# Sums of squares of the query and key heads: one exact fp32 product against two fp32r products, taken two weight pieces later

## The chip, the cores and the metric

One NeuronCore of a Trainium2 chip runs the whole program in one launch. The metric is device time in microseconds. The engines are PE (TensorE), ACT (ScalarE), DVE (VectorE), POOL (GpSimd) and SP (SyncE, which here only issues transfers). Each executes its own instruction list in order, and they meet through semaphores.

## The reference, cut to what matters

Two transformer blocks run one after the other on 256 tokens of width 2048 in float32. The change is in the first block, where the input projection gives queries and keys for two attentions of 8 heads each, and every head is normalised over its 128 elements:

```python
proj = h @ w_in
qa, ka, va, za, q_idx, k_idx, w_idx, qb, kb, vb, zb = jnp.split(proj, COL_SPLITS, axis=-1)
qa = _rms_norm(qa.reshape(heads_a), q_norm_a)
ka = _rms_norm(ka.reshape(heads_a), k_norm_a)
# the same for qb and kb
# _rms_norm: x * rsqrt(mean(x * x, axis=-1) + 1e-6) * g
```

In the kernel a head lies with its 128 elements on the 128 partitions and the 256 tokens along the free axis. The sum over the elements of a head is therefore a sum over partitions. It is made on PE, as a product of the squares with a 128x128 matrix of ones, which also puts the sum on every partition.

## The kernel before, in words

**Weights in pieces.** A projection is cut into panels of 512 output columns (4 PSUM banks of 128), and a panel into 8 pieces of 128x1024 (two blocks of 128 rows). SP loads a piece into one of 4 slots (`raw`). ACT rounds it to fp32r (`w_hi`, line 1193). DVE subtracts that from the original (`w_lo`, line 1698). PE makes three fp32r products per block and bank (lines 764 to 766), 24 for a piece. Piece j uses slot j mod 4, so ACT rounds piece j+4 when PE has released piece j, and DVE can't make `w_lo` of a piece before ACT has made its `w_hi`. PE must have `w_lo` of a piece before it starts it.

**Hooks.** All other work is put behind numbered pieces of a panel, in the instruction list of each engine. A hook at 4 on ACT stands behind ACT's rounding of piece 4. A hook at 2 on PE stands behind PE's products of piece 2. An engine which waits in a hook does not go on to its next piece.

**The stage.** The panels in question are `qk_a` (4 panels, queries and keys of the first attention), `v_a` (2), `qk_b` (4) and `v_b` (2). The results of a panel are taken out while the next panel runs. So the squares are made eight times: in panels 1 to 3 of `qk_a` (a loop of three turns), panel 0 of `v_a`, panels 1 to 3 of `qk_b` (a loop of three turns) and panel 0 of `v_b`. One time is called a turn below. It goes so:

- ACT hook 2, `stored`: copies each bank to the store and squares it into `sq` (128x1024), then frees the bank.
- PE hook 0, `qk_sums` (line 838): two products of `ones` with the halves of `sq`, in fp32, into `Y`. Each shows as two records of the trace.
- ACT hook 4, `qk_rstd`: waits for these sums (`ss_ready`), then Ln, Exp and Square over 128x1024 (lines 1207 to 1209).
- DVE hook 5, `qk_norm`: a refinement of three operations (lines 1692, 1713, 1714), then the scaling of the heads. The third operation raises `rs_ready`.

**What else stands at these places.** In `qk_a`: PE hooks 0 and 3 are index logits (line 855); ACT hooks 5 and 7 are relus of them; DVE hooks 5 and 7 sum them up (`index_sum`, in front of `qk_norm`), and DVE hooks 3 and 6 are `gate_sum` (128x2048). In `v_a` DVE has a `pick` (a step of a top-64 selection) at hooks 1, 3, 5 and 7. In `qk_b` the attention of two heads of the first kind runs as well: PE has `score` at 0, `v_rows` at 3, `probs_t` at 4 and `values` at 6; ACT has `exps` at 5 and `probs_a` at 7; DVE has `softmax_in` at 4, `softmax_out` at 6 and `probs_d` at 7. There `v_rows` writes into `Y`, and so it waits until `rs_ready` says that the refinement of the same turn has read `Y`; `probs_t` waits for `softmax_out`. In `v_b` DVE has `gate_sum` at 1, 3 and 5.

Of the kernel before, what the change touches and what calls it, by code (L numbers as in the profile page):

```python
# [28 lines left out]
P = 128  # L29
D = 2048  # L30
DC = D // P
SEQ = 256
# [128 lines left out]
def memory(nc, ctx, A):  # L161
# [6 lines left out]
    def put(name, shape, dt=FP32, offset=None):  # L168
        size = int(np.prod(shape[1:])) * 4
        here = at["o"] if offset is None else offset  # L170
        t = nc.alloc_sbuf_tensor_at(name, list(shape), dt, offset=here)
        end = here + (size + 31) // 32 * 32
        if offset is None:
            at["o"] = end
        assert end <= nc.sbuf_usable_end, name
        M.end = end
        return t
# [73 lines left out]
    M.dist = put("dist", [P, 384], offset=x + 20480)  # L251
    M.dist_sel = put("dist_selected", [P, 384], offset=x + 22016)
    M.k_idx = put("k_idx_twice", [P, SEQ], offset=x + 23552)


    M.qkv = put("qkv", [P, 24 * ROWS], offset=q0)
# [53 lines left out]
    def sem(name):  # L310
        return ctx.enter_context(nc.semaphore(name))
# [18 lines left out]
    M.y2_ready = sem("y2_ready")  # L330
    M.rs_ready = sem("rs_ready")
    M.norm_done = sem("norm_done")
    M.src_ready = sem("src_ready")
    M.ahi_ready = sem("ahi_ready")
    M.act_ready = sem("act_ready")
# [398 lines left out]
def pe_program(M, pe):  # L734
# [5 lines left out]
    def panel(job, i, after={}, acts=None, pair=None, value=None, opened={}):  # L740

        acc, ready, free = (M.acc, M.acc_ready, M.acc_free) if value is None else (M.val, M.val_ready, M.val_free)
        stored = [n + (i if pair is None else pair) for n in job.free0] if value is None else [value] * 4
        for j in range(job.J):
            s = j % SLOTS
            pe.wait_ge(M.lo_ready[s], job.raw0 + job.turn(i, j) + 1)
            if acts is not None:
                pe.wait_ge(M.act_ready, acts + job.kp * (j + 1))  # L750
            for b in job.banks:
                col = 0 if len(job.banks) == 1 else b * P
                out = acc[b][:, 0:job.N]
                if j == 0:
                    at_least(pe, free[b], stored[b])
                    if b in opened:
                        opened[b]()
                for k in range(job.kp):
                    c = job.kp * j + k
                    last = c == job.kp * job.J - 1  # L760
                    a_hi, a_lo = job.rhs(c)
                    w_hi = M.hi[s][:, k * job.cols + col:k * job.cols + col + P]
                    w_lo = M.lo[s][:, k * job.cols + col:k * job.cols + col + P]
                    pe.matmul(out, w_lo, a_hi, start=c == 0, stop=False)  # L764
                    pe.matmul(out, w_hi, a_lo, start=False, stop=False)  # L765
                    ins = pe.matmul(out, w_hi, a_hi, start=False, stop=last)  # L766
                if j == job.J - 1:
                    ins.then_inc(ready[b], 1)
            if j < job.J - 1:
                ins.then_inc(M.used[s], 1)  # L770
            for step in after.get(j, ()):
                step()
# [58 lines left out]
    panel(job["qidx1"], 0, {0: [k_idx_sums], 5: [k_idx_twice]})  # L831


    def qk_sums(stored):
        def go():
            pe.wait_ge(M.acc_free[3], stored)
            for t in range(2):
                ins = pe.matmul(M.Y[:, t * 512:(t + 1) * 512], ones[:, 0:P], M.sq[:, t * 512:(t + 1) * 512],
                                start=True, stop=True)
            ins.then_inc(M.ss_ready, 1)  # L840
        return go

# [17 lines left out]

    a = job["qk_a"]
    panel(a, 0, {0: [logits(0, 0)], 3: [logits(0, 1)]})
    with pe.Fori(0, a.n - 1) as i:
        panel(a, i + 1, {0: [qk_sums(a.free0[3] + i + 1), logits(i + 1, 0)], 3: [logits(i + 1, 1)]})
    panel(job["v_a"], 0, {0: [qk_sums(a.free0[3] + 4)]})
    panel(job["v_a"], 1)


# [50 lines left out]

    def hooks(u, k_off, norms, sums=()):  # L920
        score, v_rows, probs_t, values = unit(u, k_off, norms)
        return {0: [*sums, score], 3: [v_rows], 4: [probs_t], 6: [values]}

    b = job["qk_b"]
    k_a, k_b = 16 * SEQ, 40 * SEQ
    panel(b, 0, hooks(0, k_a, 6))
    with pe.Fori(0, b.n - 1) as i:
        panel(b, i + 1, hooks(i + 1, k_a + (i + 1) * 512, i + 7, (qk_sums(b.free0[3] + i + 1),)))
    panel(job["v_b"], 0, {0: [qk_sums(b.free0[3] + 4)]})
    panel(job["v_b"], 1)  # L930

    def gate_cols():
# [233 lines left out]
def act_program(M, act):  # L1166
# [28 lines left out]
    def panel(job, i, after={}, before={}, pair=None, part=0):  # L1195

        for j in range(job.J):
            for step in before.get(j, ()):
                step()
            split(job, i, j, pair, part)  # L1200
            for step in after.get(j, ()):
                step()
# [75 lines left out]
    act.activation(M.cc[:, 3 * CT:4 * CT], M.Y[:, 128:128 + CT], ACT.Copy)  # L1278
    act.activation(M.cc[:, 0:3 * CT], M.Y[:, 640:640 + 3 * CT], ACT.Copy).then_inc(M.cols, 1)
    act.wait_ge(M.cols, 2)  # L1280
    act.activation(M.bqkv[:, 0:8], M.c2[:, V2_QKV:V2_QKV + 8], ACT.Copy, scale=HD ** -0.5)
    act.activation(M.bqkv[:, 8:24], M.c2[:, V2_QKV + 8:V2_QKV + 24], ACT.Copy)
    ch.step(act.activation(M.bgate[:, :], M.c2[:, V2_UG + 8:V2_UG + 40], ACT.Copy, scale=0.5), wait=False)
# [5 lines left out]
        return M.act2_hi[:, PITCH * k + ROWS - n:PITCH * k + ROWS]  # L1289


    def stored(job, i, tile, func=ACT.Copy, squares=None):


        def go():
            for m in range(4):
                act.wait_ge(M.acc_ready[m], job.ready0[m] + i + 1)
                dst = M.store[:, ds(tile * SEQ + m * SEQ, SEQ)]
                ins = act.activation(dst, M.acc[m][:, 0:SEQ], func)
                if squares is not None:  # L1300
                    if m == 0:
                        act.wait_ge(M.rs_ready, squares)
                    ins = act.activation(M.sq[:, m * SEQ:(m + 1) * SEQ], M.acc[m][:, 0:SEQ], ACT.Square)
                ins.then_inc(M.acc_free[m], 1)
        return go

    q0, strip, q1 = job["qidx0"], job["strip"], job["qidx1"]
# [66 lines left out]
    def out_stored(u, at):  # L1374
        def go():
            act.wait_ge(M.o_ready, u + 1)
            act.activation(M.store[:, ds(at, 512)], M.Y[:, 512:1024], ACT.Copy).then_inc(M.o_done, 1)
        return go
# [2 lines left out]
    panel(b, 0, {2: [stored(job["v_a"], 1, 28)], 5: [exps(0)], 7: [probs_a(0)]})  # L1381
    with act.Fori(0, b.n - 1) as i:
        ch.enter(i, 2)
        panel(b, i + 1, {2: [out_stored(i, qa + i * 512), stored(b, i, 32 + i * 4, squares=i + 6)],
                         4: [qk_rstd(i + 6, i + 4)], 5: [exps(i + 1)], 7: [probs_a(i + 1)]})
        ch.leave(b.n - 1)
    panel(job["v_b"], 0, {2: [out_stored(3, qa + 3 * 512), stored(b, 3, 44, squares=9)], 4: [qk_rstd(9, 7)]})
    panel(job["v_b"], 1, {2: [stored(job["v_b"], 0, 48)]})
    za, zb = job["z_a"], job["z_b"]
    panel(za, 0, {2: [stored(job["v_b"], 1, 52)], 5: [exps(4)], 7: [probs_a(4)]})  # L1390
# [294 lines left out]
def dve_program(M, dve):  # L1685
# [114 lines left out]
    def qk_norm(count, at, gain):  # L1800
# [4 lines left out]
            stt(part, part, M.gqk[:, ds(gain, 1)], M.rs[:, :], ALU.mult, ALU.mult).then_inc(M.norm_done, 1)  # L1805
        return go

    def index_sum(u, tile, first=False):

        def go():  # L1810
            if first:
                dve.wait_ge(M.score_zero, 1)
            dve.wait_ge(M.rl_ready, 2 * u + tile + 1)
            for half in range(2):
                ch.wait()
                for t in range(2):
                    n = (t + 1) * P
                    part = M.idx_score[:, t * P:t * P + n]
                    col = t * IDX_HEADS + 2 * tile + half
                    ins = stt(part, M.relu[:, half * 384 + t * P:half * 384 + t * P + n],  # L1820
                              M.w_idx[:, ds(4 * u + col, 1)], part, ALU.mult, ALU.add)
                    if half == 0 or t == 0:
                        ch.step(ins, wait=False)
                    else:
                        ins.then_inc(M.rl_used, 1)
            dve.wait_ge(M.rl_used, 2 * u + tile + 1)
        return go
# [3 lines left out]
                 7: [index_sum(0, 1)]})  # L1831
    with dve.Fori(0, a.n - 1) as i:
        ch.enter(i, 8)
        panel(a, i + 1, {3: [gate_sum(0, i + 2, 2 * i + 4)],
                         5: [index_sum(i + 1, 0), qk_norm(i + 3, (i + 2) * 4 * SEQ, i)],
                         6: [gate_sum(1, i + 2, 2 * i + 5)], 7: [index_sum(i + 1, 1)]})
        ch.leave(a.n - 1)
# [14 lines left out]
        ch.step(dve.tensor_scalar(M.work[:, :], M.work[:, :], SENTINEL / 2, NEG, ALU.is_gt, ALU.mult))  # L1852
        ch.step(dve.tensor_tensor(M.dist_sel[:, :], M.work[:, :], M.dist[:, :], ALU.add))

    panel(job["v_a"], 0, {1: [candidates, pick], 3: [pick], 5: [qk_norm(6, 20 * SEQ, 3), pick], 7: [pick]})
    panel(job["v_a"], 1, {1: [pick], 3: [pick], 5: [pick], 7: [pick, selected]})


# [35 lines left out]
    panel(b, 0, hooks(0, 0, M.dist_sel))  # L1894
    with dve.Fori(0, b.n - 1) as i:
        ch.enter(i, 5)
        panel(b, i + 1, hooks(i + 1, 2 * i + 2, M.dist_sel, [qk_norm(i + 7, (i + 8) * 4 * SEQ, i + 4)]))
        ch.leave(b.n - 1)

    def gates(n):  # L1900
        return gate_sum(n % 2, n // 2, n)

    panel(job["v_b"], 0, {1: [gates(10)], 3: [gates(11)], 5: [gates(12), qk_norm(10, 44 * SEQ, 7)]})
    panel(job["v_b"], 1, {1: [gates(13)], 3: [gates(14)], 5: [gates(15)]})

    def gate():
# [316 lines left out]
```

## Time and profile before

| | |
|---|---|
| time, median of 3 runs | 2095.51 us (2095.13 to 2096.24) |
| profiled execution, its own time | 2093.64 us |
| its span | 2091.8 us |
| PE busy | 1980.5 us, 95% of the span |
| DVE busy | 1308.3 us, 63% |
| ACT busy | 991.2 us, 47% |
| mean granted PE clock | 0.974 |

Times of rows are microseconds from the start of the span. In a timeline row stand the start, the duration, the engine, the line, the operation and its tiles, and in brackets how long the engine was idle before it and what ended that. In a row of the chain (the work that ended last, followed back) stand the start, the time that this link held the chain, the engine and the tile. In a windows row stand the stretch, its length, then for each engine the busy time and the number of instructions, then the granted PE clock as a share of full speed, the DMA share and the GB/s. The modelled duration of a matmul overlaps the next one, so the time that PE needs is read from starts.

### The profile page before, as it was taken

The page shows a single profiled execution, that of the slowest core. Times are in us where ns is not written, and L with a number is a line of the kernel's source. Part 1 is how long each engine was busy: PE and PEld are TensorE (multiplying, and loading weights), DVE is VectorE, ACT ScalarE, POOL GpSimd, SP SyncE. Part 2 cuts the span into 40 slices and gives each one's busy share as a digit, 9 for nine tenths or more (in the row PEclk, how much of TensorE's full clock was granted, in tenths as well). Part 3 has the DMA queues.
Part 4 walks back from the last instruction along what each step waited for, and adds up shares of the span by engine and source line. Part 5 has one row for each costly group of instructions (what it writes and reads, how often), then busy time and mean ns, then how long its engine had stood idle before and what let it go on. Part 6 is the DMA issues. An engine that isn't in the chain of part 4 may idle for free.

```text
span 2091.8 us, 39050 instructions
## 1 busy us (share of the span) xinstructions
PE 1980.5 (95%) x15084; PEld 1882.8 (90%) x15084; DVE 1308.3 (63%) x1647; ACT 991.2 (47%) x1430; POOL 139.3 (7%) x149
## 2 busy tenths in 40 slices
PE   4289999999999999999999999799999999999997
PEld 2289999999998999998889999799999999988885
DVE  7886886675666544444447653676677667665554
ACT  3055555554645544444444544644454454444443
POOL 0000000000002000000004111000001000000000
PEclk8599999999999999999999999899999999999999
DMA  9966664474455455544444555256555655655553
GB/s 376 355 204 239 246 200 158 159 283 146 151 188 182 151 180 165 177 141 143 140 138 151 201 183 180 72 187 200 186 170 179 200 183 170 204 208 189 191 191 121
DMA packets 179903, 391.62 MB, mean 187 GB/s; under 512 B 11955, under 2 KB 17632, under 8 KB 177376
## 3 DMA queue, kind: packets, MB, share of 16 engines
q1 hardware_dynamic: 178800, 388.03, 55.5%
q10 hardware_dynamic: 1024, 2.51, 0.3%
q8 instruction: 54, 0.88, 0.2%
q14 instruction: 25, 0.20, 0.0%
HBM read 388.39 MB, written 2.10 MB: 187 GB/s over the span
## 4 chain that ended last, share of the span: by engine, by line
PE 90%; DVE 6%; ACT 2%; issue 1%; DMA 1%; SPq 0%; DVEq 0%; POOLq 0%; POOL 0%; ACTq 0%
PE acc L764 21%; PE acc L765 20%; PE acc L766 20%; PE psum_x L764 2%; PE psum_y L765 2%; PE psum_x L765 2%; PE psum_x L766 2%; PE psum_y L766 2%; PE psum_y L764 2%; DVE ada_acc L1692 2%; PE acc L1145 2%; PE acc L1144 2%; PE acc L1146 2%; DVE ada_first L1692 2%; PE psum_y L1145 1%
## 5 line engine op out<-in xcount | busy, mean ns | idle before, releaser
L1698 DVE TENSOR_TENSOR w_lo<-raw,w_hi 128x1024 fp32r<-128x1024 f32 (+1 forms) x644 | 810.0, 1271 | 655.2 <-ACT w_hi L1193 652.5
L1193 ACT ACTIVATE w_hi<-raw 128x1024 fp32r<-128x1024 f32 (+1 forms) x644 | 672.6, 1051 | 837.0 <-PE acc L766 547.6
L764 PE MATMUL acc<-act_hi,w_lo 128*128 128x258 f32 (+2 forms) x3424 | 976.1, 285 | 19.3 <-issue 11.1
L765 PE MATMUL acc<-act_lo,w_hi 128*128 128x258 f32 (+2 forms) x3424 | 965.3, 282 | 0.0
L766 PE MATMUL acc<-act_hi,w_hi 128*128 128x258 f32 (+2 forms) x3424 | 965.0, 282 | 0.0
L764 PEld LDWEIGHTS acc<-act_hi,w_lo 128*128 128x128 f32 x3424 | 648.9, 190 | 30.5 <-issue 28.7
L765 PEld LDWEIGHTS acc<-act_lo,w_hi 128*128 128x128 f32 x3424 | 648.0, 189 | 0.7 <-issue 0.5
L766 PEld LDWEIGHTS acc<-act_hi,w_hi 128*128 128x128 f32 x3424 | 648.1, 189 | 0.0
L764 PE MATMUL psum_x<-act_hi,w_lo 128*128 128x258 f32 x352 | 99.8, 283 | 4.1 <-DVE w_lo L1698 4.1
L765 PE MATMUL psum_x<-act_lo,w_hi 128*128 128x258 f32 x352 | 99.6, 283 | 0.0
L764 PE MATMUL psum_y<-act_hi,w_lo 128*128 128x258 f32 x352 | 99.6, 283 | 0.0
L765 PE MATMUL psum_y<-act_lo,w_hi 128*128 128x258 f32 x352 | 99.6, 283 | 0.0
L766 PE MATMUL psum_x<-act_hi,w_hi 128*128 128x258 f32 x352 | 99.6, 283 | 0.0
L766 PE MATMUL psum_y<-act_hi,w_hi 128*128 128x258 f32 x352 | 99.6, 283 | 0.0
L764 PEld LDWEIGHTS psum_x<-act_hi,w_lo 128*128 128x128 f32 x352 | 66.9, 190 | 4.5 <-DVE w_lo L1698 4.5
L725 POOL TENSOR_TENSOR ffn_act<-gelu_gate,conv_val 128x1024 f32 x11 | 35.2, 3201 | 524.6 <-DVE conv_val L1692 524.6
L1145 PE MATMUL acc<-w_lo,down_hi 128*128 128x512 f32 x176 | 69.3, 394 | 0.0
L1144 PE MATMUL acc<-w_hi,down_lo 128*128 128x512 f32 x176 | 69.0, 392 | 0.0
L1146 PE MATMUL acc<-w_hi,down_hi 128*128 128x512 f32 x176 | 68.3, 388 | 0.0
L765 PEld LDWEIGHTS psum_x<-act_lo,w_hi 128*128 128x128 f32 x352 | 66.9, 190 | 0.0
L765 PEld LDWEIGHTS psum_y<-act_lo,w_hi 128*128 128x128 f32 x352 | 66.8, 190 | 0.0
L766 PEld LDWEIGHTS psum_y<-act_hi,w_hi 128*128 128x128 f32 x352 | 66.8, 190 | 0.0
(296 smaller groups left out, 2207.8 us busy)
## 6 DMA issues: line engine op xcount, KB each, us to landing
raw<-in_w_in SPq DMA_DIRECT2D x272, 512.0 KB, 3.5
raw<-in_w_ffn_up SPq DMA_DIRECT2D x176, 512.0 KB, 4.4
raw<-in_w_ffn_down SPq DMA_DIRECT2D x88, 512.0 KB, 3.6
raw<-in_w_out SPq DMA_DIRECT2D x64, 512.0 KB, 4.1
raw<-in_w_ada SPq DMA_DIRECT2D x32, 512.0 KB, 8.3
ada_w<-in_w_ada SPq DMA_DIRECT2D x32, 512.0 KB, 8.0
ada_x<-in_w_ada SPq DMA_DIRECT2D x16, 1024.0 KB, 6.2
raw<-in_w_attn_o SPq DMA_DIRECT2D x16, 512.0 KB, 3.6
```

Of the source, the lines that this page charges most:

```text
L725: pool.tensor_tensor(M.F[:, ds(i * 4 * SEQ, 4 * SEQ)], M.gg[:, :], M.vt[:, :], ALU.mult).then_inc(M.F_ready, 1)
L764: pe.matmul(out, w_lo, a_hi, start=c == 0, stop=False)
L765: pe.matmul(out, w_hi, a_lo, start=False, stop=False)
L766: ins = pe.matmul(out, w_hi, a_hi, start=False, stop=last)
L1144: pe.matmul(out, d_lo, w_hi, start=start, stop=False)
L1145: pe.matmul(out, d_hi, w_lo, start=False, stop=False)
L1146: ins = pe.matmul(out, d_hi, w_hi, start=False, stop=stop)
L1193: act.activation(M.hi[s][:, 0:job.width], M.raw[s][:, 0:job.width], ACT.Copy).then_inc(M.hi_ready[s], 1)
L1692: return dve.scalar_tensor_tensor(out, in0, scalar, in1, op0, op1)
L1698: dve.tensor_tensor(M.lo[s][:, 0:job.width], M.raw[s][:, 0:job.width], M.hi[s][:, 0:job.width].bitcast(FP32), ALU.subtract).then_inc(M.lo_ ...
```

## The change

Four things are done, each eight times.

- ACT, at the end of `stored`, copies `sq` rounded to fp32r into a new tile `sq_hi` (128x1024). Before it, it waits for its own last square.
- DVE has a new hook at 2, `square_low`: it waits for that copy and subtracts it from `sq`, giving `sq_lo` (128x1024, fp32r).
- PE makes, for each half, two fp32r products of a rounded matrix of ones, with `sq_lo` and with `sq_hi`, in place of the fp32 product. That is four products with 512 columns.
- These products stand at PE hook 2 in place of hook 0, and wait for `square_low` in place of the freed bank.

The hooks of `qk_rstd` (ACT 4) and `qk_norm` (DVE 5) stay. Once, early in the program, ACT makes the rounded ones. The new tiles lie in parts of the store that are empty at the time. No transfer is added or moved.

```diff
-    def qk_sums(stored):
+    def qk_sums(n, side):
         def go():
-            pe.wait_ge(M.acc_free[3], stored)
+            pe.wait_ge(M.sql_ready, n + 1)
             for t in range(2):
-                ins = pe.matmul(M.Y[:, t * 512:(t + 1) * 512], ones[:, 0:P], M.sq[:, t * 512:(t + 1) * 512],
-                                start=True, stop=True)
+                out, part = M.Y[:, t * 512:(t + 1) * 512], slice(t * 512, (t + 1) * 512)
+                pe.matmul(out, M.ones_r[:, :], M.sq_lo[side][:, part], start=True, stop=False)
+                ins = pe.matmul(out, M.ones_r[:, :], M.sq_hi[side][:, part], start=False, stop=True)
             ins.then_inc(M.ss_ready, 1)
...
-        panel(a, i + 1, {0: [qk_sums(a.free0[3] + i + 1), logits(i + 1, 0)], 3: [logits(i + 1, 1)]})
-    panel(job["v_a"], 0, {0: [qk_sums(a.free0[3] + 4)]})
+        panel(a, i + 1, {0: [logits(i + 1, 0)], 2: [qk_sums(i, 0)], 3: [logits(i + 1, 1)]})
+    panel(job["v_a"], 0, {2: [qk_sums(3, 0)]})
...
-        return {0: [*sums, score], 3: [v_rows], 4: [probs_t], 6: [values]}
+        return {0: [score], 2: list(sums), 3: [v_rows], 4: [probs_t], 6: [values]}
...
-        panel(b, i + 1, hooks(i + 1, k_a + (i + 1) * 512, i + 7, (qk_sums(b.free0[3] + i + 1),)))
-    panel(job["v_b"], 0, {0: [qk_sums(b.free0[3] + 4)]})
+        panel(b, i + 1, hooks(i + 1, k_a + (i + 1) * 512, i + 7, (qk_sums(i + 4, 1),)))
+    panel(job["v_b"], 0, {2: [qk_sums(7, 1)]})
...
+    act.activation(M.ones_r[:, :], M.ones[:, 0:P], ACT.Copy).then_inc(M.ones_ready, 1)
...
+            if squares is not None:
+                act.wait_ge(M.acc_free[3], job.free0[3] + i + 1)
+                act.activation(M.sq_hi[side][:, :], M.sq[:, :], ACT.Copy).then_inc(M.sqh_ready, 1)
...
+    def square_low(n, side):
+
+        def go():
+            dve.wait_ge(M.sqh_ready, n + 1)
+            dve.tensor_tensor(M.sq_lo[side][:, :], M.sq[:, :], M.sq_hi[side][:, :].bitcast(FP32), ALU.subtract
+                              ).then_inc(M.sql_ready, 1)
+        return go
...
-        panel(a, i + 1, {3: [gate_sum(0, i + 2, 2 * i + 4)],
+        panel(a, i + 1, {2: [square_low(i, 0)], 3: [gate_sum(0, i + 2, 2 * i + 4)],
```

The hook of `square_low` at 2 is added in the same way in panel 0 of `v_a`, in the loop of `qk_b` and in panel 0 of `v_b`.

## Rows read from the trace of the kernel before

**Rows 1.** The windows: one turn of `qk_a` and one of `qk_b`.

```profile
192.58:218.21 25.63, 25.63 (x213) 23.60 (x213) 21.34 (x23) 15.37 (x21) 1.19 (x1) 1.00 0.56 205
...
369.67:398.65 28.98, 28.13 (x223) 26.62 (x223) 18.81 (x26) 17.11 (x29) 1.72 (x2) 1.00 0.46 145
```

**Rows 2.** The chain in a turn of `qk_a`: sums, logits, three pieces, logits.

```profile
192.58 1.72 PE psum_y L838 x4
194.29 0.86 PE psum_x L855 x8
...
203.53 0.86 PE psum_x L855 x8
```

**Rows 3.** The timeline of ACT in the same turn.

```profile
196.64 1.07 ACT L1209 ACTIVATE squares<-rstd 128x1024 f32<-128x1024 f32 x1
198.19 1.06 ACT L1193 ACTIVATE w_hi<-raw 128x1024 fp32r<-128x1024 f32 x1 [0.48 <-PE acc L766]
```

**Rows 4.** The timeline of DVE in the same turn.

```profile
199.28 1.23 DVE L1698 TENSOR_TENSOR w_lo<-raw,w_hi 128x1024 fp32r<-128x1024 f32 x1 [2.88 <-ACT w_hi L1193]
...
202.09 1.22 DVE L1692 SCALAR_TENSOR_TENSOR squares<-psum_y,squares 128x1024 f32<-128x1024 f32 x1
...
206.78 1.21 DVE L1698 TENSOR_TENSOR w_lo<-raw,w_hi 128x1024 fp32r<-128x1024 f32 x1
...
213.38 3.50 DVE L1698 TENSOR_TENSOR w_lo<-raw,w_hi 128x1024 fp32r<-128x1024 f32 x3 [0.44 <-DVE idx_score L1692]
```

**Rows 5.** The page's costliest groups: the subtraction and the rounding of a piece.

```profile
L1698 DVE TENSOR_TENSOR w_lo<-raw,w_hi 128x1024 fp32r<-128x1024 f32 (+1 forms) x644 | 810.0, 1271 | 655.2 <-ACT w_hi L1193 652.5
L1193 ACT ACTIVATE w_hi<-raw 128x1024 fp32r<-128x1024 f32 (+1 forms) x644 | 672.6, 1051 | 837.0 <-PE acc L766 547.6
```

**Rows 6.** The windows: 20 us of the last stage, fp32r products of 512 columns.

```profile
1900.00:1920.00 20.00, 20.00 (x89) 16.39 (x89) 9.65 (x11) 9.13 (x12) 0.00 (x0) 1.00 0.53 187
```

**Rows 7.** The timeline of ACT in panel 0 of `v_a`.

```profile
273.52 1.06 ACT L1209 ACTIVATE squares<-rstd 128x1024 f32<-128x1024 f32 x1
274.49 1.05 ACT L1193 ACTIVATE w_hi<-raw 128x1024 fp32r<-128x1024 f32 x1
```

**Rows 8.** The timeline of DVE in panel 0 of `v_a`.

```profile
275.57 1.23 DVE L1698 TENSOR_TENSOR w_lo<-raw,w_hi 128x1024 fp32r<-128x1024 f32 x1 [1.08 <-ACT w_hi L1193]
276.71 1.22 DVE L1692 SCALAR_TENSOR_TENSOR squares<-psum_y,squares 128x1024 f32<-128x1024 f32 x1
...
282.85 2.36 DVE L1698 TENSOR_TENSOR w_lo<-raw,w_hi 128x1024 fp32r<-128x1024 f32 x2
```

**Rows 9.** The timeline of DVE in panel 0 of `v_b`.

```profile
434.47 2.35 DVE L1692 SCALAR_TENSOR_TENSOR ada_acc<-ada_x,silu_c,ada_acc 128x2048 f32<-128x2048 f32 x1
...
441.18 5.04 DVE L1698 TENSOR_TENSOR w_lo<-raw,w_hi 128x1024 fp32r<-128x1024 f32 x4
```

**Rows 10.** The chain in a turn of `qk_b`.

```profile
371.38 1.31 PE psum_x L881 x8
372.69 0.12 PE acc L764
...
377.85 1.23 DVE squares L1692
...
379.83 1.24 DVE rstd L1714
...
382.54 1.63 DVE w_lo L1698
...
385.36 0.88 PE psum_x L775 x6
```

**Rows 11.** The windows: two idle stretches of PE, and PE's work right behind each.

```profile
1307.81:1314.17 6.36, 0.00 (x1) 0.03 (x1) 4.74 (x10) 3.09 (x8) 0.00 (x0) 0.77 0.00 0
1314.17:1318.05 3.88, 3.88 (x18) 3.88 (x19) 3.81 (x7) 1.91 (x4) 0.00 (x0) 0.50 0.01 2
1349.57:1353.70 4.13, 0.00 (x0) 0.00 (x1) 1.28 (x2) 4.00 (x7) 0.00 (x0) 0.82 0.00 0
1353.70:1359.02 5.32, 5.32 (x24) 5.32 (x25) 4.63 (x9) 4.25 (x7) 0.00 (x0) 0.50 0.31 99
```

More of the change, by code:

```diff
@@ L253, in memory @@
     M.k_idx = put("k_idx_twice", [P, SEQ], offset=x + 23552)
+    M.ones_r = put("ones_rounded", [P, P], F32R, x + 24576)
+    M.sq_hi = [put(f"squares_hi{n}", [P, 4 * SEQ], F32R, store(part)) for n, part in enumerate((4, 0))]
+    M.sq_lo = [put(f"squares_lo{n}", [P, 4 * SEQ], F32R, store(part) + 4096) for n, part in enumerate((4, 0))]
     M.qkv = put("qkv", [P, 24 * ROWS], offset=q0)
@@ L332, in memory @@
     M.norm_done = sem("norm_done")
+    M.ones_ready = sem("ones_ready")
+    M.sqh_ready = sem("sqh_ready")
+    M.sql_ready = sem("sql_ready")
     M.src_ready = sem("src_ready")
@@ L862, in pe_program @@
     panel(a, 0, {0: [logits(0, 0)], 3: [logits(0, 1)]})
+    pe.wait_ge(M.ones_ready, 1)
     with pe.Fori(0, a.n - 1) as i:
-        panel(a, i + 1, {0: [qk_sums(a.free0[3] + i + 1), logits(i + 1, 0)], 3: [logits(i + 1, 1)]})
-    panel(job["v_a"], 0, {0: [qk_sums(a.free0[3] + 4)]})
+        panel(a, i + 1, {0: [logits(i + 1, 0)], 2: [qk_sums(i, 0)], 3: [logits(i + 1, 1)]})
+    panel(job["v_a"], 0, {2: [qk_sums(3, 0)]})
     panel(job["v_a"], 1)
@@ L1289, in hi2_of, with stored @@
         return M.act2_hi[:, PITCH * k + ROWS - n:PITCH * k + ROWS]
-    def stored(job, i, tile, func=ACT.Copy, squares=None):
+    def stored(job, i, tile, func=ACT.Copy, squares=None, side=0):
         def go():
@@ L1383, in act_program @@
         ch.enter(i, 2)
-        panel(b, i + 1, {2: [out_stored(i, qa + i * 512), stored(b, i, 32 + i * 4, squares=i + 6)],
+        panel(b, i + 1, {2: [out_stored(i, qa + i * 512), stored(b, i, 32 + i * 4, squares=i + 6, side=1)],
                          4: [qk_rstd(i + 6, i + 4)], 5: [exps(i + 1)], 7: [probs_a(i + 1)]})
         ch.leave(b.n - 1)
-    panel(job["v_b"], 0, {2: [out_stored(3, qa + 3 * 512), stored(b, 3, 44, squares=9)], 4: [qk_rstd(9, 7)]})
+    panel(job["v_b"], 0, {2: [out_stored(3, qa + 3 * 512), stored(b, 3, 44, squares=9, side=1)], 4: [qk_rstd(9, 7)]})
     panel(job["v_b"], 1, {2: [stored(job["v_b"], 0, 48)]})
@@ L1853, in selected @@
         ch.step(dve.tensor_tensor(M.dist_sel[:, :], M.work[:, :], M.dist[:, :], ALU.add))
-    panel(job["v_a"], 0, {1: [candidates, pick], 3: [pick], 5: [qk_norm(6, 20 * SEQ, 3), pick], 7: [pick]})
+    panel(job["v_a"], 0, {1: [candidates, pick], 2: [square_low(3, 0)], 3: [pick], 5: [qk_norm(6, 20 * SEQ, 3), pick], 7: [pick]})
     panel(job["v_a"], 1, {1: [pick], 3: [pick], 5: [pick], 7: [pick, selected]})
@@ L1896, in dve_program @@
         ch.enter(i, 5)
-        panel(b, i + 1, hooks(i + 1, 2 * i + 2, M.dist_sel, [qk_norm(i + 7, (i + 8) * 4 * SEQ, i + 4)]))
+        panel(b, i + 1, {2: [square_low(i + 4, 1)],
+                         **hooks(i + 1, 2 * i + 2, M.dist_sel, [qk_norm(i + 7, (i + 8) * 4 * SEQ, i + 4)])})
         ch.leave(b.n - 1)
@@ L1901, in gates @@
         return gate_sum(n % 2, n // 2, n)
-    panel(job["v_b"], 0, {1: [gates(10)], 3: [gates(11)], 5: [gates(12), qk_norm(10, 44 * SEQ, 7)]})
+    panel(job["v_b"], 0, {1: [gates(10)], 2: [square_low(7, 1)], 3: [gates(11)], 5: [gates(12), qk_norm(10, 44 * SEQ, 7)]})
     panel(job["v_b"], 1, {1: [gates(13)], 3: [gates(14)], 5: [gates(15)]})
```

## The prediction

> **What bounds the kernel now.** I read the page first. PE is busy for 95% of the span, so a microsecond that PE loses in this stage is lost at the end too, unless it shortens an idle stretch that PE has anyway. Then I took the windows from sums to sums. In a turn of `qk_a` PE is busy for all of the 25.63 us and DVE for 21.34; in a turn of `qk_b` PE has less than 1 us idle in 28.98 [rows 1]. Then came the chain: in `qk_a` it stays on PE [rows 2], and in `qk_b` it leaves PE once a turn, for ACT's rounding and then DVE's refinement, `w_lo` and softmax, until PE can transpose the probabilities [rows 10]. Last I read the timelines of ACT and DVE, to see who is how late in a turn. The question for this change is how much slack lies between the end of the sums (called S below) and the first piece on PE that needs what ACT and DVE do behind their hooks 4 and 5.
>
> **PE's own work.** Before, the fp32 sums hold PE for 1.72 us [rows 2]. The four new products have 512 columns, and fp32r products of that width come 89 in 20 us, 0.225 us each [rows 6]: 0.90 us. That gives back 0.82 us a turn. The bounds: not under four products of half the width (72 of them fill the 8.38 us of three pieces below, 0.116 each: 0.47 us), and not over the 1.72 of the fp32 form, so between 0 and 1.25 us a turn. I take 0.82, since the rows have the same type and width.
>
> **The added passes.** ACT's copy is as large as a rounding, 1.05 us, and DVE's subtraction as a `w_lo`, 1.27 us with its spread [rows 5]. They stand before the split of piece 3, and PE needs that only after its pieces 0 to 2, some 8 us later. In `qk_a` DVE's busy time would go from 21.34 to about 22.5 of 24.8 us. I cost both at nothing while pieces 1 and 2 cover them; without cover they would cost 2.3 us a turn. The rounded ones are made once, long before the stage, and cost nothing.
>
> **The move is what costs.** On ACT hook 4 `qk_rstd` waits for the sums, and behind it on ACT stands the rounding of piece 5. Before, the sums end at 194.29 [rows 2], ACT begins its last step of `rstd` at 196.64, and the rounding of piece 5 comes at 198.19, released by PE and not by `rstd` [rows 3]. The wait was free. Now the sums end two pieces later, and ACT stands still at hook 4 with piece 5 unrounded, DVE behind it. From S on all turns share a chain:
> - S to the rounding of piece 5: 2.35 us to the Square (194.29 to 196.64, rows 2 and 3), then 0.97 [rows 7]: S+3.32.
> - DVE takes up `w_lo` of piece 5 1.08 later, S+4.40, and is through 1.14 later [rows 7, 8]: S+5.54.
>
> After S, PE has work for piece 3, piece 4 and piece 5. In `qk_a` three pieces last 195.15 to 203.53, 8.38 us [rows 2].
>
> **A turn of `qk_a` (three).** DVE needs 2.81 us from `w_lo` 5 over `index_sum` to `qk_norm` and 4.69 more until `w_lo` of piece 6 starts [rows 4]: S+11.90, ready at S+13.17. PE has 8.38 and the logits' 0.86 [rows 2], so it arrives at S+9.24 and waits 3.93 us. DVE stays late: `w_lo` of the next panel's piece 0 starts 6.60 after that of piece 6 [rows 4], ready at S+19.75, while PE would be there two pieces (5.5) after S+13.17; another 1.1 us. With the 0.82 back: 4.2 us a turn, 12.6 for three.
>
> **`v_a` (one).** From S+5.54 DVE needs 6.14 for `qk_norm` and `pick` (276.71 to 282.85, rows 8): `w_lo` 6 ready at S+12.95. PE has 8.38, waits 4.57; net 3.75.
>
> **A turn of `qk_b` (three).** The refinement starts at S+5.54 and its third step ends 3.21 later (377.85 to 379.83, and 1.23, rows 10): S+8.75. `v_rows` behind piece 3 waits for it. PE comes there at S+2.8, so it waits 5.9 us. The rest of the chain, 4.69 to `w_lo` and 2.82 to the transposes [rows 10], sets `probs_t` at S+13.05. Before, it stood at S+13.98 (371.38 to 385.36), but with `score` (1.31) and pieces 1 and 2 (5.6) between. These 6.9 us now stand ahead of S, so a turn changes by 13.05 - 13.98 + 6.9 - 0.82 = 5.15, 15.5 for three.
>
> **`v_b` (one).** From S+5.54, `gate_sum` and `qk_norm` take 6.71 [rows 9]: `w_lo` 6 ready at S+13.5, PE waits 5.1, net 4.3.
>
> Sum at full clock: 12.6 + 3.75 + 15.5 + 4.3 = 36.2 us. Bounds: with the products at either bound it is 32.8 to 42.8. No link of it is a resource that the trace does not show.
>
> **The clock.** PE stands idle for 6.36 us and for 4.13 us near 1310 and 1350. In both the granted clock falls before PE goes on, and PE then works 3.88 and 5.32 us at 0.50, which is 1.2 GHz and not 2.4 [rows 11]. Half of that, 1.9 to 2.7 us, is lost; I take 2.3. The waits of `v_a`, `qk_b` and `v_b` (4.6, 5.9, 5.1) are longer than 4.13, so I count a fall in each. Those of `qk_a` (3.9) are a little shorter; I count one in two. What it costs: in `v_a` and `v_b` the full 2.3. In `qk_b`, `v_rows` and piece 4 end at S+14.4 and not S+12.1, past the 13.05 of `probs_t`: 1.35 a turn, 4.05. In `qk_a` the slow piece hides the second wait of 1.1: 1.2 a turn, 1.8 for three at one in two. Together 10.45; bounds: 0 without any fall, 15.5 with 2.7 lost at each of eight.
>
> The Trainium skill ("TensorE: Matmul & The Clock Gate", section "HAM oscillation — how this bites in real kernels") says that a kernel whose matmuls wait once in each iteration can fall back to the slow clock every time. By it every one of the eight waits has a fall; by the rows alone that is sure for five. It speaks against a change that makes waits.
>
> **Forecast.** 36.2 + 10.45 = 46.6 us. Against the profiled execution, 2093.64, that gives 2140.3; the median of the runs is 1.87 above it, so 2095.51 + 46.6 = 2142.1 us.
>
> **Rivals.**
> - *Clock stays up.* The waits are there, but PE's dense work around them keeps the clock. For it: the idle stretches of rows 11 stand beside small fp32 products, those here between dense pieces. Against: they are as long. 36.2 us: 2131.7.
> - *A fall at each of the eight.* 46.6 + 1.8 = 48.4: 2143.9, and with the longer slow stretches (2.7) 2148. That is inside the forecast's own range.
> - *Late loads on top.* SP issues the load of a slot when `w_lo` has left it, so DVE's lateness makes loads late. It decides if a piece lands after ACT could round it. The DMA share in these turns is 0.46 to 0.56 [rows 1], which speaks against. At 1 us a turn: +8, 2150.
> - *The other side: the chain has slack that I don't see.* If PE found `w_lo` 6 and `rs_ready` on time, only the 0.82 of each turn would be left: 8 x 0.82 = 6.6, 2088.9. It decides where ACT's hook 4 would have to end two pieces earlier than S+3.3, and nothing in the change moves that hook. The same comes out if the busy share were the judge (DVE 22.5 of 24.8 us).
> - *Partly hidden.* DVE or ACT save some of the chain because they have less to do while PE waits: the waits at full clock are 36.2 + 6.6 = 42.8 us, half of them less the 6.6 is +14.8, 2110.3.
>
> **How the numbers follow.** Forecast with five to eight falls 0.60 (its own range 2137 to 2149); clock stays up 0.20; late loads 0.10; partly hidden 0.07; waits all hidden 0.03. The range takes in the second and most of the third: 2127 to 2152. A difference under 0.2% (4.2 us) can't be told from none. Slower by more has all but the last case and a rest: 0.96; no change 0.01; faster 0.03.
>
> **What would show each step.** Each PE group of line 838's successor holds PE for 0.9 us. ACT is idle some 5 us before Ln in each turn, released by PE's sums. PE is idle near 4 us before piece 6 in `qk_a`, released by `w_lo`; near 5.9 us before `v_rows` in `qk_b`, released by DVE's `rstd`. The turn of `qk_a` is 30 to 31 us, that of `qk_b` 34 to 35.5. The clock shows 0.50 behind the waits. The forecast is wrong if ACT rounds piece 5 without waiting for the sums, or if the granted clock stays at 1.00.

## The result, and the profile after

The changed kernel takes 2140.65 us (median of 4 runs, 2138.72 to 2142.02) against 2095.32 for the kernel before. The ratio is 1.0218, with a 95% interval of 1.0205 to 1.0231: 45 us slower. Its profiled execution has a span of 2136.9 us, where before had 2091.8, and a mean granted clock of 0.967, where before had 0.974. PE's busy share fell from 95% to 93%. All ratios here and below are of fast runs; of the kernels below one run, 2229 us at a granted clock of 0.83, was in the chip's slow state.

First the waits of PE in the stage, from 180 to 520 us: who waited for whom, the total, how often, and the longest.

```profile
PE psum_y L781 <- DVE rstd L1726: 17.8, 3, 5.9
PE acc L770 <- DVE w_lo L1710: 13.7, 9, 4.7
PE psum_x L862 <- ACT relu_logits L1351: 6.8, 3, 2.3
```

Before, PE waited 2.1 us for the probabilities here and hardly for anything else. Now it waits 38.3 us. The first row is `v_rows` in the three turns of `qk_b`, 5.9 us each. The second is mostly piece 6 (4.7 us in `v_b`, 4.3 in `v_a`, 0.4 to 1.6 in the turns of `qk_a`). The third is one that the prediction did not name: the second index logits of `qk_a`, 2.3 us in each of its turns.

Second, ACT in the first turn of `qk_a`, in the timeline; these answer to [rows 3].

```profile
201.03 1.12 ACT L1215 ACTIVATE rstd<-psum_y,eps_col 128x1024 f32<-128x1024 f32 x1 [6.38 <-PE psum_y L846]
...
203.27 1.06 ACT L1217 ACTIVATE squares<-rstd 128x1024 f32<-128x1024 f32 x1
204.23 1.04 ACT L1201 ACTIVATE w_hi<-raw 128x1024 fp32r<-128x1024 f32 x1
205.18 0.79 ACT L1351 ACTIVATE relu_logits<-psum_x 128x768 f32<-128x768 f32 x1
```

Before, the last step of `rstd` was followed by a rounding that PE released. Now the bracket of Ln shows 6.38 us of idleness (forecast some 5; over the eight turns it is 46.7 us, 5.8 each), ended by PE's sums, and the rounding of piece 5 comes straight behind the Square, 3.3 us after the sums (which end at 200.93).

Third, DVE in the same turn; these answer to [rows 4].

```profile
205.30 1.23 DVE L1710 TENSOR_TENSOR w_lo<-raw,w_hi 128x1024 fp32r<-128x1024 f32 x1 [6.86 <-ACT w_hi L1201]
...
212.95 1.22 DVE L1710 TENSOR_TENSOR w_lo<-raw,w_hi 128x1024 fp32r<-128x1024 f32 x1
...
219.56 3.50 DVE L1710 TENSOR_TENSOR w_lo<-raw,w_hi 128x1024 fp32r<-128x1024 f32 x3 [0.44 <-DVE idx_score L1704]
```

Counted from S = 200.93, `w_lo` of piece 5 starts at S+4.37 (forecast S+4.40), of piece 6 at S+12.02 (S+11.90), of the next piece 0 at S+18.63 (S+18.5).

Fourth, the sums in the chain. After, the first link of the four products of each turn; then before, all four records of a turn in one link (its first turn stands in [rows 2]).

```profile
200.00 0.23 PE psum_y L845
230.44 0.23 PE psum_y L845
260.84 0.23 PE psum_y L845
289.65 0.23 PE psum_y L845
...
368.70 0.23 PE psum_y L845
403.17 0.23 PE psum_y L845
437.49 0.23 PE psum_y L845
472.14 0.23 PE psum_y L845
```

```profile
218.21 1.72 PE psum_y L838 x4
243.83 1.72 PE psum_y L838 x4
269.46 1.72 PE psum_y L838 x4
...
340.76 1.72 PE psum_y L838 x4
...
369.67 1.72 PE psum_y L838 x4
398.65 1.72 PE psum_y L838 x4
427.22 1.72 PE psum_y L838 x4
```

From one row to the next, after less before, is +4.81, +4.78, +3.18, +7.75, +5.56, +5.34 and +6.08 us. The sums moved past the logits (0.86 us) or `score` (1.31 us), so three of these have to be put right: `v_a` has no logits, so the third is 4.04; the fourth has a `score` more, so it is 6.44; `v_b` has no `score`, so the last is 7.39. `qk_a` is then the first three, `v_a` the fourth, `qk_b` the next three. For `v_b` the landmark behind the last sums is PE's wait of 4.7 us for a `w_lo` (it ends at 678.44 before and at 721.92 after):

| part | forecast | measured in the trace |
|---|---|---|
| `qk_a`, three turns | 12.6 + 1.8 | 13.6 |
| `v_a` | 3.75 + 2.3 | 6.4 |
| `qk_b`, three turns | 15.5 + 4.05 | 18.3 |
| `v_b`, up to the landmark | 4.3 + 2.3 | 4.2 |
| ahead of the stage | 0 | 0.9 |
| behind the landmark | 0 | 1.6 |
| sum | 46.6 | 45.1 |

The 45.1 is the difference of the spans. The 1.6 behind the landmark lies where the two programs are the same. Of the 0.9 ahead of the stage, PE's wait for the first sums of the modulation (20.7 us, before 19.8) is the visible part. The move alone, below, also waits 19.8 us there, and every kernel with the rounded ones 20.2 to 20.7; whether making them lengthens this wait was not tried.

### The profile page after: what moved, and what is told of

Same layout as the page of the kernel before. It is cut to its first block, busy times and chain, and to the rows that moved or that the text cites. A ratio compares the mean times of both kernels' runs of the same rounds, so it can differ in the third digit from the quotient of the medians.

```text
span 2136.9 us, 39073 instructions
## 1 busy us (share of the span) xinstructions
PE 1987.6 (93%) x15084; PEld 1894.3 (89%) x15084; DVE 1317.3 (62%) x1655; ACT 996.5 (47%) x1439; POOL 139.0 (7%) x149
## 4 chain that ended last, share of the span: by engine, by line
PE 87%; DVE 7%; ACT 2%; issue 2%; DMA 1%; DVEq 0%; SPq 0%; POOLq 0%; POOL 0%; ACTq 0%
PE acc L770 20%; PE acc L771 20%; PE acc L772 20%; DVE ada_acc L1704 2%; PE psum_x L770 2%; PE psum_x L771 2%; PE psum_x L772 2%; PE psum_y L772 2%; PE psum_y L771 2%; PE psum_y L770 2%; PE acc L1153 2%; PE acc L1152 2%; PE acc L1154 2%; DVE ada_first L1704 1%; DVE w_lo L1710 1%
## 5 line engine op out<-in xcount | busy, mean ns | idle before, releaser
L770 PE MATMUL acc<-act_hi,w_lo 128*128 128x258 f32 (+2 forms) x3424 | 981.3, 287 | 33.5 <-DVE w_lo L1710 13.7
L772 PEld LDWEIGHTS psum_x<-act_hi,w_hi 128*128 128x128 f32 x352 | 66.8, 190 | 0.0
```

## The experiments

Every kernel ran beside the kernel before on one chip, and its ratio is against that.

**The move alone.** The two fp32 products of before at hook 2, with no copy, no subtraction and no new products.

```diff
# against the kernel before
-        panel(a, i + 1, {0: [qk_sums(a.free0[3] + i + 1), logits(i + 1, 0)], 3: [logits(i + 1, 1)]})
+        panel(a, i + 1, {0: [logits(i + 1, 0)], 2: [qk_sums(a.free0[3] + i + 1)], 3: [logits(i + 1, 1)]})
# the same move in v_a, in the loop of qk_b and in v_b
```

> The move alone: the two fp32 products of before, at PE hook 2 in place of hook 0, with no copy and no subtraction. Theory A (the late sums hold ACT at hook 4, and piece 5 behind it): all waits of the changed kernel are still there, and each of the eight sums is 0.82 us longer, so 45 + 6.6 = 52 us slower than before, 2147 us, and no faster than 2142. Theory B (the added passes on ACT and DVE make the weights late, the place of the sums does not matter): as before, 2095 us. PE idle before the logits at hook 3 in qk_a about 2.3 us, before v_rows in qk_b about 5.9 us under A, none under B.

Measured: 2146.73 us, ratio 1.0241 (1.0222 to 1.0261), 50 us slower than before. The waits of PE:

```profile
PE psum_y L775 <- DVE rstd L1714: 18.1, 3, 6.0
PE acc L764 <- DVE w_lo L1698: 13.8, 11, 4.8
PE psum_x L855 <- ACT relu_logits L1339: 7.1, 3, 2.4
```

They are the three rows of the changed kernel, within 0.3 us each. The move makes them; the split into rounded squares and remainder is not needed for them.

**One piece earlier.** The changed kernel with its sums at hook 1.

```diff
-    ... 2: [qk_sums(i, 0)], ...   2: [qk_sums(3, 0)]   2: list(sums)   2: [qk_sums(7, 1)]
+    ... 1: [qk_sums(i, 0)], ...   1: [qk_sums(3, 0)]   1: list(sums)   1: [qk_sums(7, 1)]
```

> The changed kernel with its sums at PE hook 1, one piece earlier than hook 2. Theory A: the sums end one piece (2.75 us) and in qk_a nothing else earlier, so every wait shrinks by about that: in qk_a 1.3 us at piece 6 and 1.0 at the next piece 0, less 0.82, is 1.5 a turn; in v_a and v_b 1.0 and 1.6; in qk_b 2.35 a turn with v_rows 3.1 us late. Sum 14 us: 2109, up to 2116 if the clock falls in the waits of qk_b. Theory B: no difference to hook 2, 2140.

Measured: 2113.98 us, ratio 1.0082 (1.0061 to 1.0102), 17 us slower. The waits:

```profile
PE psum_y L781 <- DVE rstd L1726: 9.4, 3, 3.1
PE acc L770 <- DVE w_lo L1710: 8.7, 10, 2.2
```

`v_rows` waits 3.1 us a turn as forecast, and the time lies between the 2109 without and the 2116 with a fall of the clock. The cost follows the place. In its trace the clock falls behind two of the three waits of 3.1 us, and not behind the one that ends at 396.35.

**Back at hook 0.** The changed kernel with only the move undone.

```diff
-        panel(a, i + 1, {0: [logits(i + 1, 0)], 2: [qk_sums(i, 0)], 3: [logits(i + 1, 1)]})
+        panel(a, i + 1, {0: [qk_sums(i, 0), logits(i + 1, 0)], 3: [logits(i + 1, 1)]})
# the same in v_a, qk_b and v_b
```

> The changed kernel with its sums back at PE hook 0, so the copy, the subtraction and the four fp32r products are kept and only the move is undone. Theory A: the place is the cost. In qk_a PE waits about 0.9 us for the subtraction, which eats the 0.82 that the products give back; in qk_b the same. 2095 (2092 to 2098). Theory B (the passes cost): 2120 or more.

Measured: 2097.14 us, ratio 1.0014 (1.0003 to 1.0025), 3 us slower than before and 43 faster than the change. In its trace PE waits for the remainder:

```profile
PE psum_y L845 <- DVE squares_lo L1824: 5.0, 8, 2.2
```

The 6.6 us of shorter products were to meet some 7 us of waits, and 5.0 are recorded. In `v_a`, where `pick` stands in front of the subtraction on DVE, the wait is 2.2 us. The gain is eaten up all the same, and the trace shows three causes. First, each recorded wait holds PE some 0.27 us longer than its bracket says (last section): eight times, 2.2 us. Second, the wait of 2.2 us has a stretch at half clock behind it, and the stretch that the kernel before has in `v_b` (shown further down) is twice as long here; PE works 10.2 us at half clock in the stage where before had 3.4, which costs 3.4 us more:

```profile
274.20:277.60 3.40, 3.40 (x16) 3.21 (x15) 3.14 (x8) 2.30 (x3) 0.00 (x0) 0.50 0.82 267
...
482.40:489.20 6.80, 6.80 (x33) 6.80 (x33) 2.35 (x7) 0.00 (x0) 0.00 (x0) 0.50 0.25 77
```

Third, two of its turns have products at a wider spacing, 1.6 us (last section). From the first sums to the landmark, with seven of the eight waits in it, the trace is 5.35 us longer than before; the parts give 4.6 + 1.9 + 3.4 + 1.6 - 6.6 = 4.9. It is the trace of one execution, of 2100.86 us, 3.7 above the median; how much of the last two causes the others have is not recorded.

**The passes alone.** Copy and subtraction are made and not used; the sums are those of before, at hook 0.

```diff
# against the changed kernel; qk_sums and its places are those of before
+            act.wait_ge(M.sql_ready, ss - 1)
             rstd(M.ss_ready, ss, M.Y[:, :], M.rs[:, :], M.sq[:, :], HD)
```

> The copy on ACT and the subtraction on DVE are made but not used; the sums are the fp32 products of before at hook 0. ACT waits for the subtraction before its Ln, which comes later anyway. Theory A: both passes lie under pieces 0 to 2, 2095 (2094 to 2098). Theory B: they cost up to 2.3 us a turn and what follows from it, 2114 or more.

Measured: 2095.72 us, ratio 1.0011 (0.9995 to 1.0026). The span of its profiled execution is 2091.5, and PE's waits in the stage are the 2.1 us of before. Sixteen passes of 1.0 to 1.3 us add no wait of PE; the interval of the times alone leaves room for up to 5.4 us.

**Half of the change.** `qk_a` and `v_a` changed, `qk_b` and `v_b` as before.

```diff
# against the changed kernel
-        return {0: [score], 2: list(sums), 3: [v_rows], 4: [probs_t], 6: [values]}
+        return {0: [*sums, score], 3: [v_rows], 4: [probs_t], 6: [values]}
# with the fp32 products in these sums, and without copy and square_low in qk_b and v_b
```

> The change in qk_a and v_a alone; qk_b and v_b have the fp32 sums at hook 0 and no added passes. Theory A: three turns of +4.8 us and v_a with a wait of 4.7 us less 0.82 and about 1.5 for the clock, 19 to 20 us slower than before, 2115. If instead the slowdown sits in qk_b, where attention shares the engines (each turn 5.5 there and nothing in qk_a), it is under 5 us slower, 2100.

Measured: 2115.35 us, ratio 1.0091 (1.0072 to 1.0111): 19 us. By difference the other 26 belong to `qk_b` and `v_b`. The forecast's parts are 20.5 and 26.2.

**The second logits later.** In `qk_a`, from PE hook 3 to hook 5.

```diff
-        panel(a, i + 1, {0: [logits(i + 1, 0)], 2: [qk_sums(i, 0)], 3: [logits(i + 1, 1)]})
+        panel(a, i + 1, {0: [logits(i + 1, 0)], 2: [qk_sums(i, 0)], 5: [logits(i + 1, 1)]})
```

> The changed kernel with the second logits of qk_a at PE hook 5 in place of hook 3. In the changed kernel PE waits 2.3 us there for a relu that stands behind piece 5 on ACT, and then 1.6 us at piece 6. Theory A with DVE's chain as the limit: the first wait goes and the one at piece 6 becomes 4 us, the turn stays at 30.4 us, 2140 us (2138 to 2144, more if the longer wait makes the clock fall in turns 2 and 3). Rival (the wait at the logits is a cost of its own, on top): each of three turns is 2.3 us shorter, 2134.

Measured: 2144.31 us, ratio 1.0228 (1.0208 to 1.0248), and no gain. The waits of PE in the stage, then the one at piece 6 in the second turn of `qk_a`, then a window behind it:

```profile
PE acc L770 <- DVE w_lo L1710: 19.8, 5, 4.7
PE psum_y L781 <- DVE rstd L1726: 17.9, 3, 6.0
```

```profile
244.37 0.58 PE L770 MATMUL acc<-act_hi,w_lo 128*128 128x256 f32 x1 [3.60 <-DVE w_lo L1710]
```

```profile
244.50:249.00 4.50, 4.50 (x27) 4.50 (x28) 4.36 (x6) 0.00 (x1) 0.00 (x0) 0.65 0.43 121
```

The wait at the logits is gone and the one at piece 6 has grown to 3.6 us. The first two turns last 30.4 and 30.5 us from sums to sums, as in the changed kernel (30.4 both). So DVE's chain sets the turn, and PE waits in front of it at the one place or at two. The undivided wait has a fall of the clock behind it in all three turns, where the changed kernel has one in the first alone. The rival fell.

**Everything that stands on the sums moves with them, except in `qk_b`.** There the sums are at hook 0.

```diff
# ACT, qk_a (v_a and v_b alike)
-                         4: [qk_rstd(i + 2, i)],
-                         5: [relus(2 * i + 2)], 7: [relus(2 * i + 3)]})
+                         5: [relus(2 * i + 2), qk_rstd(i + 2, i)], 7: [relus(2 * i + 3)]})
# DVE, qk_a (in v_a and v_b qk_norm moves from 5 to 6)
-                         5: [index_sum(i + 1, 0), qk_norm(i + 3, (i + 2) * 4 * SEQ, i)],
-                         6: [gate_sum(1, i + 2, 2 * i + 5)], 7: [index_sum(i + 1, 1)]})
+                         5: [gate_sum(1, i + 2, 2 * i + 5), index_sum(i + 1, 0)],
+                         6: [qk_norm(i + 3, (i + 2) * 4 * SEQ, i)], 7: [index_sum(i + 1, 1)]})
```

> The sums stay at hook 2 in qk_a, v_a and v_b, and what stands on them moves too: ACT's rstd from hook 4 to the end of hook 5, DVE's qk_norm from 5 to 6, with the second gate_sum of qk_a from 6 to 5. In qk_b the sums are at hook 0 and the rest is as before. Theory A: ACT has piece 5 rounded before it waits, and piece 6 is ready 5.6 us behind the sums where PE needs it 8.4 us behind, so no wait is left in the first three; five turns give back 0.82 each and qk_b is as in the run with all sums at hook 0: 2091 (2089 to 2095). If ACT's hook were not the cause, 2115 or more.

Measured: 2092.55 us, ratio 0.9988 (0.9977 to 0.9998). The sums are at hook 2 in five of eight turns and no wait for `w_lo` is left. So hook 2 itself is not the fault; it is the hooks behind it that stayed. ACT's hook and DVE's were moved together, and what ACT's alone would give back was not tried.

**The same in `qk_b`.**

```diff
# the loop of qk_b, against the run before
# PE:  {0: sums, score; 3: v_rows; 4: probs_t; 6: values}  ->  {0: score; 2: sums; 4: probs_t; 5: v_rows; 6: values}
# ACT: {4: qk_rstd; 5: exps; 7: probs_a}                   ->  {4: exps; 5: qk_rstd; 6: probs_a}
# DVE: {4: softmax_in; 5: qk_norm; 6: softmax_out, copy of v_rows; 7: probs_d}
#                                ->  {4: softmax_in; 5: softmax_out; 6: qk_norm, copy of v_rows, probs_d}
```

> As the run before, and in the loop of qk_b the sums stay at hook 2 as well: ACT has exps at 4, rstd at 5, probs_a at 6; DVE has softmax_out at 5, then qk_norm, the copy of v_rows and probs_d at 6; PE has probs_t at 4, v_rows at 5, values at 6. Theory A: eight sums give back 0.82 each and the 2.1 us that PE waited for the probabilities before are gone: 2087 (2085 to 2092). Rival (DVE's longer list in qk_b becomes the limit): over 2095.

Measured: 2086.44 us, ratio 0.9961 (0.9945 to 0.9977), 8 us faster than before and 54 faster than the change. In the stage PE waits for nobody. ACT in the first turn of `qk_a`, then a turn of `qk_b` in the windows:

```profile
196.94 1.06 ACT L1203 ACTIVATE w_hi<-raw 128x1024 fp32r<-128x1024 f32 x1 [2.73 <-PE acc L772]
...
200.59 1.12 ACT L1217 ACTIVATE rstd<-psum_y,eps_col 128x1024 f32<-128x1024 f32 x1 [1.89 <-PE psum_y L846]
```

```profile
347.13:374.20 27.07, 27.07 (x224) 26.69 (x223) 19.17 (x26) 17.90 (x31) 2.64 (x2) 1.00 0.49 156
```

Piece 5 is rounded at 196.94, and only then does ACT wait, 1.89 us and for nothing that PE needs. A turn of `qk_b` is 27.1 us, where before had 28.98 [rows 1] and the change has 34.5.

**That order with the old products.**

```diff
# against the run before: qk_sums with fp32 and M.sq; no copy, no square_low
```

> The order of the last run (sums at hook 2, all that stands on them later), but with the two fp32 products of before in place of copy, subtraction and four fp32r products. If the gain of that order is the 2.1 us of waits in qk_b, and the products' gain is 0.82 us a turn as read from the trace, this kernel is 6.6 us slower than the last run and 2.1 faster than before: 2093 (2090 to 2095). If the products give back nothing once the waits are gone, it is as fast as the last run, 2086.

Measured: 2093.35 us, ratio 0.9998 (0.9989 to 1.0007); its span is 2091.2, that of the run before 2084.4. The two kernels differ by 6.9 us in their medians and 6.8 in their spans: eight times 0.82 is 6.6. They ran on two chips, and by their ratios to before the difference is 7.7 us, give or take 4. The traces narrow it: from the first sums to the landmark behind `v_b` they differ by 6.1 us, from sums to sums by 0.6 to 1.0 a turn. So the cheaper products are worth about what was read from the rows, once nothing takes it back. What the order alone gives, forecast at 2.1, is not told from nothing by the ratio (-2.3 to +1.5 us).

## Why the prediction was right

The mechanism was right, and the chain behind the sums came out within 0.2 us of what was read from the rows. That the sum is only 1.5 us off is in part luck: the clock was wrong in its parts, a cost of each wait was left out, `qk_b` and `v_b` were taken too dear and `v_a` too cheap, and 2.5 us of the difference lie outside the stage.

**PE's own work** (0.82 back a turn) held. The links of the four products are 0.23 each, 0.93 us for the four, which gives back 0.79. The traces of the last two experiments put the eight turns at 6.1 us for 6.6.

**The added passes** (nothing) held: the run with the passes alone has no more waits than before, and the move alone is no faster than the change.

**The move** held, with its chain. S+3.3, S+4.4 and S+12 were measured at 3.3, 4.37 and 12.02. The move alone costs 50 us, the changed kernel with the move undone 3, and with the followers moved too it is 8 faster than before.

**A turn of `qk_a`** had the right size and one wrong place. The wait of 3.93 us at piece 6 was missed as such: the second logits of PE stand at hook 3 and wait for a relu that stands behind piece 5 on ACT. The timeline of PE in the first turn and in the second:

```profile
206.02 0.93 PE L862 MATMUL psum_x<-k_idx_twice,q_idx_staged 64*128 64x128 f32 x8 [2.26 <-ACT relu_logits L1351]
...
217.62 0.39 PE L770 MATMUL acc<-act_hi,w_lo 128*128 128x256 f32 x1 [0.39 <-DVE w_lo L1710]
```

```profile
236.45 0.93 PE L862 MATMUL psum_x<-k_idx_twice,q_idx_staged 64*128 64x128 f32 x8 [2.26 <-ACT relu_logits L1351]
...
244.65 0.38 PE L770 MATMUL acc<-act_hi,w_lo 128*128 128x256 f32 x1 [1.61 <-DVE w_lo L1710]
```

In the second turn it is 2.26 and 1.61 us, 3.87 in all for 3.93. That the sum is DVE's is shown by the run with the later logits. What the turn left out is smaller: every wait costs PE some 0.27 us beyond its bracket (last section), and the changed kernel has 15 waits in the stage where before had 4, so 3 us in all.

**`qk_b`**: `v_rows` waited 5.95 us for 5.9, and in the first turn `probs_t` came at S+13.7 (383.32 after 369.62) for 14.4.

```profile
378.40 1.12 PE psum_y L781 x4
...
383.32 0.66 PE psum_x L781 x6
```

**The clock** was forecast at 10.45 us. Here is the first turn of `qk_a`, then the first and the third of `qk_b`, and `v_b`; they answer to [rows 11]:

```profile
206.02:211.05 5.03, 5.03 (x30) 4.70 (x31) 4.78 (x8) 2.65 (x3) 0.61 (x1) 0.66 0.34 104
...
372.45:378.40 5.95, 0.00 (x1) 0.01 (x1) 4.28 (x4) 5.16 (x12) 0.00 (x0) 0.69 0.28 88
378.40:381.50 3.10, 3.10 (x15) 3.10 (x16) 2.88 (x3) 0.00 (x0) 0.64 (x1) 0.50 0.02 5
...
447.19:453.30 6.11, 6.11 (x29) 6.11 (x30) 5.25 (x9) 0.00 (x0) 0.00 (x0) 0.50 0.62 232
...
486.56:490.80 4.24, 4.24 (x20) 4.24 (x21) 4.24 (x4) 0.00 (x0) 0.42 (x1) 0.50 0.69 194
```

In all PE works at half clock for 3.4 us in the first turn of `qk_a`, 3.0 in `v_a`, 3.2, 2.8 and 6.1 in `qk_b` and 4.2 in `v_b`. Half of it is lost, 1.4 to 3.0 us a time where 2.3 was taken, 11.4 in all. So there are six falls, and two turns of `qk_a` without one. The fall in the first turn hides in DVE's lateness (30.4 us, like the second turn, which has none), so the 1.8 us counted there came out near nothing. The third turn of `qk_b`, with the longest stretch, grew by 7.4 us where its neighbours grew by 5.6 and 5.3; the forecast had 6.5 for each.

What the forecast did not see is that the kernel before has a fall of its own in this stage, in the last panel of `v_b`, without any idle time of PE. Right ahead of it PE makes 32 products of one column. The row of its timeline, then the window:

```profile
474.96 3.68 PE L936 MATMUL psum_y<-ones,ada_acc 128*128 128x1 f32 x32
```

```profile
478.40:481.80 3.40, 3.40 (x17) 3.40 (x17) 2.35 (x7) 0.00 (x0) 0.00 (x0) 0.50 0.23 89
```

The changed kernel makes the same products from 519.88 on and has no fall there: from 490.80 to 540.00 its granted clock is 1.00. So in `v_b` one fall took the place of another, and of the 2.3 us counted 0.4 are left. That is most of why `v_b` measured 4.2 us and not 6.6. Net of this the clock cost 9.7 us.

The rule cited from the Trainium skill (TensorE: Matmul & The Clock Gate, section "HAM oscillation — how this bites in real kernels") agrees for six of the eight turns (half clock behind or in the wait); for the second and third turn of `qk_a`, where the granted clock is 1.00 throughout, this trace does not agree.

One sum in the prediction is off by little: with 2.7 us lost at each of the eight waits the rival's time is 36.2 + 15.5 above 2095.51, 2147 us and not 2148.

The rivals: the clock did not stay up; no late load shows among PE's waits in the stage; the waits were neither hidden nor halved. Both the forecast and its second rival (a fall at each of the eight, 2143.9) lie near the measured time, and the number alone does not tell them apart; the granted clock does.

## What to carry to other kernels

A consumer that stands at a fixed place in an engine's list keeps everything behind it waiting, also the work that feeds the engine which is to release it. So when a producer is moved back by two pieces, its consumers have to be moved as far, and the price is read by counting on from the new end of the producer: here some 5 us a turn against 0.8 us of gain. A wait that the trace of before shows as free says only that the order was right for the place it had.

## What the runs showed of the hardware

The same length of waiting made the clock fall in one turn and not in another. 2.26 us idle ahead of the logits are followed by a granted clock of 0.66 over the next 5 us in the first turn of `qk_a`; the second turn, with the same 2.26 and 1.61 more, has 1.00 throughout, and so has the third:

```profile
231.36:261.76 30.40, 25.86 (x215) 24.10 (x214) 22.38 (x23) 16.39 (x22) 0.61 (x1) 1.00 0.59 213
```

With the sums at hook 1, PE's wait of 3.13 us in `qk_b` has a clock of 0.50 behind it in the first turn (364.83 to 367.60) and 1.00 in the second (396.20 to 400.00). And a fall needs no idle time at all, as the kernel before shows at 478.40. Whether its 32 products of one column have a part in it stays open: in the kernel with everything moved later the clock falls 0.8 us after the first of them, and in the changed kernel it does not fall.

A wait costs PE more than its bracket. In the rows below the last product ahead of the wait starts at 219.29 and the first behind it at 219.94, 0.65 later, where 0.12 is usual: 0.53 us for a bracket of 0.37. The next product follows 0.34 later where 0.23 is usual. That is 0.27 us beyond the bracket, and the starts around the waits of 1.6 and 2.26 us in the changed kernel give the same 0.16 ahead of the first product.

PE's fp32r products of 256 columns have two spacings at full clock. In the timeline of the run with the sums back at hook 0, and then of the kernel before at the same place, first and last of a run of products (the rows between them are left out):

```profile
218.35 0.28 PE L770 MATMUL acc<-act_hi,w_lo 128*128 128x256 f32 x1
...
219.29 0.28 PE L772 MATMUL acc<-act_hi,w_hi 128*128 128x256 f32 x1
219.94 0.50 PE L845 MATMUL psum_y<-squares_lo,ones_rounded 128*128 128x512 f32 x1 [0.37 <-DVE squares_lo L1824]
220.28 0.39 PE L846 MATMUL psum_y<-squares_hi,ones_rounded 128*128 128x512 f32 x1
```

```profile
217.36 0.28 PE L764 MATMUL acc<-act_hi,w_lo 128*128 128x256 f32 x1
...
217.93 0.28 PE L766 MATMUL acc<-act_hi,w_hi 128*128 128x256 f32 x1
```

The first are eight steps in 0.94 us, 0.118 each; the second five steps in 0.57, 0.114 each. A kernel stays at one of them for whole stretches: by the starts, the first two turns of `qk_a` have a mean of 0.1177 us there and the third 0.1134, and the kernel before has 0.1135 in all three. Over the 192 products of a turn that is about 0.8 us, as much as the whole gain of the cheaper sums; it is the last of the three causes for which that run wins nothing (its first two turns are 26.3 us, 219.94 less 193.65, for 25.6). In its other turns the spacing is that of before or closer, up to the last sums. What puts PE into the one or the other was not tried and stays open.
